# Filler products of a hybrid decoder kernel moved from the paired delta rule and its sample tile to the end of the chunked mixers

## The chip, the cores and the metric

The kernel runs on one core of one Trainium2 chip. The metric is the device time of one execution in microseconds (us); lower is better. All operands are float32.

## The reference, cut to what matters

One inference step of a trunk of two layers (DEPTH = 2) for 512 prompt tokens and 8 x 4 = 32 sample tokens, with width 1024. Each layer projects the tokens once and feeds four groups of heads, then mixes them, attends to a memory and applies an MLP:

```
z = x @ P['w_in']                               # 1024 -> N_IN, split among the groups
hm, C1, n1, m1 = _mlstm(...)                    # A: chunked matrix memory
ro, R1 = _retention(_rotary(rq), _rotary(rk), rv, R0)   # B: chunked retention
hg, h1, conv1 = _rglru(...)                     # C: gated linear recurrence
y_w, S1, shift1 = _rwkv7(...)                   # D: delta rule, per step
mix = concat([y_m, y_r, y_g, y_w]) @ P['w_out']
x = LN(ALPHA * x + mix); x = LN(ALPHA * x + cross_attn(x)); x = LN(ALPHA * x + mlp(x))
kp = mem_prompt @ xa_wk[l]; vp = mem_prompt @ xa_wv[l]   # memory keys and values
```

The delta rule D is, per head and time step, `S = S*w - (S kk) (kk*a)^T + v k^T; o = S r`. The kernel computes it in chunks of 64 tokens, with the inverse of a triangular matrix built by doubling.

## The kernel before, in words

**Tokens and tiles.** The 544 tokens are five tiles: T = 0 to 3 hold 128 prompt tokens each, T = 4 the 32 sample tokens. A projection column block f (128 output features) is kept as z(f), features on partitions, tokens along the row, and is made in two halves: 256 and 288 tokens.

**Two kinds of work on TensorE.** Every layer has a latency-bound stage, in which TensorE issues small matmuls for the groups D, A and B and waits between them for ScalarE, VectorE or GpSimd to turn their results into the next operands. To fill these waits the kernel holds back dense products that nothing near by needs and issues them in small portions: the fillers. They are needed work, listed in `SPARE` (line 708) in a fixed order: first 24 halves of z (slabs 4, 5 and 6 of `w_in`, column blocks 4 to 15), of 8 products each, then 16 halves of the memory keys and values (slabs 7 to 10, `xa_wk` and `xa_wv`), also of 8 products each. `spare_products` (line 723) issues the next ones at a named point of the program; its `units` count a z product (line 738, 128x256 or 128x288) as one and a key or value product (line 735, 128x512) as two. In the trace every product is two MATMUL records: one unit of z is two records of L738, two units of keys are two records of L735. The number of units at each point is written by hand:

- `FILL_OM` (3): ahead of the first level of an inverse (line 1076). `FILL_X` (5): at each level from m = 2 on (line 1090), between the product X and the products D and DT that need X back from ScalarE.
- lines 1055 and 1059 (3 and 5): while the scores of a tile of D are prepared, for each of the five tiles.
- line 1122 (3, and 1 for T = 4), line 1138 (1), `FILL_ST` (3, line 1146) and `FILL_SA` (2, line 1165): around the recurrence over the chunks.
- the sample tile of D, lines 1197 to 1247; then `FILL_D`, `FILL_BC`.
- `FILL_AB`: in the chunked mixers A and B, for each T, one portion between `front(T + 1)` and the scores of B (line 1421) and one after `outputs("A", T, 0)` (line 1424).
- `FILL_AB_S` (4): twice in each of the sample outputs of A and B (lines 1349 and 1353).

**Order of the work.** `delta_scores`, `delta_inverse`, `delta_states` run for the tile groups (0, 1), (2, 3) and (4,) (lines 1262 ff.). A paired group (g = 0, 1) inverts 8 heads x 2 chunks at once over the levels m = 1, 2, 4, 8, 16, 32; the sample tile (g = 2) has the levels 1 and 2. Level m begins with the product X (L1085), which needs a mask product of GpSimd (L2167) and the matrix Dm that VectorE writes (L1674 for m = 1, L1679 after it). ScalarE copies X back (L2022), TensorE makes D and DT (L1099, L1105), VectorE subtracts them (L1679, L1681). In the recurrence TensorE makes SA (L1155), VectorE turns it (L1699), TensorE uses it (L1173). For T = 4 VectorE also prepares the rotary embedding (L1609 to L1611) and spreads the values (L1724, L1726) that TensorE needs for the sample state (L1240).

In the mixers `outputs` for T = 4 multiplies the stored states with 4 tokens at a time: 32 records of 64x4 (L1345) for each half of the heads. A's needs the normalised output of the tile before (VectorE, L1803), whose PSUM bank it takes over.

**Banks and drains.** A filler half owns one PSUM bank from its first product until ScalarE has copied it out (L1922 for z, L1928 for keys and values). In the mixers all halves of keys and values use bank 3, so the first product of a half waits until the half before is copied. ScalarE looks for finished halves at fixed points (`spare_tiles`), in the order in which `HALF_DONE` says that they are finished.

**Loads.** SyncE issues the loads of the slabs into two ring slots, each when the slab two before it has been consumed (`slab_read`); these waits stand in SyncE's one queue, with the stores of states and the loads of the sample states between them.

Of the kernel before, what the change touches and what calls it, by code (L numbers as in the profile page):

```python
# [224 lines left out]
def build(nc, A, O, table, where):  # L225

    with ExitStack() as ctx:
# [130 lines left out]
        for l in range(DEPTH):  # L358
# [127 lines left out]
            UV = cols(tmp, dbase + 2048, H, HD)  # L486
# [224 lines left out]
            HALF_DONE = {}  # L711

            FILL_BONUS = 2 * KC
            FILL_OM, FILL_X, FILL_ST, FILL_SA = 3, 5, 3, 2
            FILL_4 = 4
            KV_BANKS = (0, 3)
            FILL_D = (4, 10)
            FILL_BC = 4
            FILL_AB = (6, ((6, 4), (10, 6), (10, 6), (10, 6)))
            FILL_AB_S = 4  # L720


            def spare_products(pe, point, units, banks, upto=None):

                at = HALF_DONE.get("at", 0)
                while at < len(SPARE) and (units > 0 if upto is None else at < upto):
                    n, f, half, k = SPARE[at]
                    key = ("kv", n - 7, half) if f is None else ("z", f, half)
                    if k == 0:
                        if half == 0 and (f is None or f == SLABS_IN[n][1]):  # L730
                            slab_pe(pe, n)
                        bk.begin(pe, key, banks[half] if f is not None or banks[0] == 3 else KV_BANKS[half])
                    bank = psum[:, bk.turn[key][0], :]
                    if f is None:
                        ins = pe.matmul(bank, memT[:, k, half * P:(half + 1) * P], wring[:, n % 2, k, :], start=(k == 0), stop=(k == KC - 1))  # L735
                    else:
                        c, i = HALVES[half][1], f - SLABS_IN[n][1]
                        ins = pe.matmul(bank[:, :c.stop - c.start], wring[:, n % 2, k, i * P:(i + 1) * P], xTv[:, k, c],  # L738
                                        start=(k == 0), stop=(k == KC - 1))
                    if k == KC - 1:  # L740
                        bk.filled(ins, key)
                    units -= 2 if f is None else 1
                    at += 1
                HALF_DONE["at"] = at
                HALF_DONE[point] = at // KC
# [214 lines left out]
            with nc.Block() as block:  # L960

                @block.tensor
                def _(pe):
# [40 lines left out]
                    for part, c in HALVES:  # L1004
                        w = c.stop - c.start
                        ps = bk.begin(pe, ("gates", "part", part), 4 + part)
                        for k in range(KC):
                            g = (k % 4) * NS
# [34 lines left out]
                    def delta_scores(T):  # L1043

                        t0, n = TILES[T]
                        dpad = dpads[T % 2]
                        own_chunks = CHUNKS if T < 4 else (slice(0, NS),)
                        pe.wait_ge(sig["dfeat"], sig.at("dfeat", 1))
                        for i, pair in enumerate(((X2, X4), (z(ZK_D, 2), z(ZV_D, 2)))):
                            ps = bk.begin(pe, ("dtok", T, i), (5, 7)[i]).rearrange("p (a c) -> p a c", a=4)  # L1050
                            for j in range(2):
                                for pr in range(2):
                                    ins = pe.transpose(ps[:n, 2 * j + pr, :], pair[j][:, pr, t0:t0 + n], ident)
                            bk.filled(ins, ("dtok", T, i))
                        spare_products(pe, ("dpad", T), 3, (0, 1))
                        pe.wait_ge(sig["dpad"], sig.at("dpad", 2 * (T + 1)))
                        for i, left in enumerate((X4, z(ZK_D, 2))):
                            if i:
                                spare_products(pe, ("dsc", T), 5, (0, 1))
                            ps = bk.begin(pe, ("dsc", T, i), (6, 4)[i]).rearrange("p (q a s t) -> p q a s t", q=2, a=2, s=2)  # L1060
                            for pr in range(2):
                                for c in own_chunks:
                                    tc = slice(t0 + c.start, t0 + c.stop)
                                    w = c.stop - c.start
                                    ins = pe.matmul(ps[c, pr, :, :, :w], left[:, pr, tc], dpad[:, pr, :, :, c], start=True, stop=True)
                            bk.filled(ins, ("dsc", T, i))


                    def delta_inverse(g):

                        tiles, levels = TILE_GROUPS[g], GROUP_LEVELS[g]
                        own_chunks = CHUNKS if g < 2 else (slice(0, NS),)
                        heads = range(H * len(tiles))
                        for li, m in enumerate(levels):
                            last = m == levels[-1]
                            spare_products(pe, ("om", g, m), FILL_OM if m == 1 or g == 2 else 0, (0, 1))
                            pe.wait_ge(sig["om"], sig.at("om", OM0[g] + li + 1))
                            ps = bk.begin(pe, ("X", g, m), 2).rearrange("p (h t) -> p h t", h=2 * H)
                            om = OmT[:, (OM0[g] + li) % 2]
                            if m > 1:  # L1080
                                bk.given(pe, ("X", g, 1) if m == 2 else ("D", g, m // 2))
                            for h in heads:
                                for c in own_chunks:
                                    w = c.stop - c.start
                                    ins = pe.matmul(ps[c, h, :w], om[c, h, :w], (const("ident64") if m == 1 else Dm[:, h, :])[c, :w],  # L1085
                                                    start=True, stop=True)
                            bk.filled(ins, ("X", g, m))
                            if m == 1:
                                continue
                            spare_products(pe, ("X", g, m), FILL_X, (0, 1))  # L1090
                            bk.given(pe, ("X", g, m))
                            if m > 2:
                                bk.given(pe, ("DT", g, m // 2))
                            if not last:
                                ps = bk.begin(pe, ("D", g, m), 3).rearrange("p (h t) -> p h t", h=2 * H)
                                for h in heads:
                                    for c in own_chunks:
                                        w = c.stop - c.start
                                        ins = pe.matmul(ps[c, h, :w], DmT[c, h, :w], Xm[c, h, :w], start=True, stop=True)  # L1099
                                bk.filled(ins, ("D", g, m))  # L1100
                            ps = bk.begin(pe, ("DT", g, m), 4).rearrange("p (h t) -> p h t", h=2 * H)
                            for h in heads:
                                for c in own_chunks:
                                    w = c.stop - c.start
                                    ins = pe.matmul(ps[c, h, :w], Xm[c, h, :w], DmT[c, h, :w], start=True, stop=True)  # L1105
                            bk.filled(ins, ("DT", g, m))


                    def delta_states(T):

                        t0, n = TILES[T]
                        dpad, Dtok, h0 = dpads[T % 2], Dtoks[T % 2], H * (T % 2)
# [6 lines left out]
                                ins = pe.matmul(ps[c, h, :], KM[c, h0 + h, 0, :c.stop - c.start],  # L1119
                                                Dtok[c, 3, h // 2, (h % 2) * HD:(h % 2) * HD + HD], start=True, stop=True)  # L1120
                        bk.filled(ins, ("CV", T))
                        spare_products(pe, ("inv", T), 3 if T < 4 else 1, (0, 1))
                        bk.given(pe, ("DT", T // 2, GROUP_LEVELS[T // 2][-1]))
                        if T < 4:
                            for cc, c in enumerate(CHUNKS):
# [9 lines left out]
                                for c in CHUNKS:  # L1135
                                    ins = pe.matmul(ps[c, 2 * (h % 2) + h // 2, :], DmT[c, h0 + h, :], CV[c, h, :], start=True, stop=True)
                            bk.filled(ins, ("UV", T))
                            spare_products(pe, ("UV", T), 1, (0, 1))
                            bk.given(pe, ("WK", T, 0))
                            bk.given(pe, ("WK", T, 1))  # L1140
                            bk.given(pe, ("UV", T))
# [186 lines left out]
                    def outputs(pre, T, bank):  # L1328
# [11 lines left out]
                        if T == 4:  # L1340
                            for pr in range(2):
# [6 lines left out]
                                if pr == 0:  # L1348
                                    spare_products(pe, ("ab", pre, 0), FILL_AB_S, (3, 3))
                            if pre == "A":  # L1350
# [65 lines left out]
                    key_scores("B", 0, 6)  # L1416
                    spare_products(pe, ("ab", 0, 0), FILL_AB[0], (3, 3))
                    for T in range(4):
                        outputs("B", T, 2)
                        front(T + 1)  # L1420
                        spare_products(pe, ("ab", T, 1), FILL_AB[1][T][0], (3, 3))
                        key_scores("B", T + 1, 6)
                        outputs("A", T, 0)
                        spare_products(pe, ("ab", T, 2), FILL_AB[1][T][1], (3, 3))
                    outputs("A", 4, 0)
# [907 lines left out]
            inv = cols(tmp, 10248, 4)  # L2333
# [894 lines left out]
```

## Time and profile before

| | |
|---|---|
| median of the runs | 2240.8 us (3 runs, 2239.32 to 2241.57) |
| profiled execution, its own time | 2243.67 us |
| span of the profiled execution | 2241.8 us |
| mean granted TensorE clock | 0.992 |
| TensorE busy with matmuls | 2188.2 us, 98% of the span |
| VectorE busy | 1167.9 us, 52% |
| ScalarE busy | 427.9 us, 19% |
| GpSimd busy | 113.0 us, 5% |
| DMA | 217.30 MB, mean 97 GB/s |

How to read it: times in a trace are us from the start of the span. PE is TensorE, DVE VectorE, ACT ScalarE, POOL GpSimd, SP SyncE. Matmuls are pipelined: a record's duration is longer than the distance to the next one, so neighbouring records overlap, and a busy PE is not a PE at its peak. What a group of records costs TensorE is the distance from its start to the start of the next group. "Granted clock" is the share of the full TensorE clock (2.4 GHz) that the chip granted; 0.50 is its lower level, 1.2 GHz. The latency-bound stage lies at 162 to 450 us in the first layer and at 1270 to 1556 us in the second.

### The profile page before, as it was taken

What the parts mean: (1) busy time and instruction counts of PE and PEld (TensorE: products, weight loads), DVE (VectorE), ACT (ScalarE), POOL (GpSimd) and SP (SyncE); (2) the same over time, 40 slices, a digit from 0 to 9 for tenths busy, and PEclk for the clock granted to TensorE, in tenths of its full rate; (3) what the DMA queues carried; (4) which work ended last, traced back from release to release, by engine and by line L of the source; (5) the groups of instructions that cost most, each with busy time, mean ns of one, the idle gap of its engine ahead of it and who ended that gap; (6) DMA issues with size and microseconds to landing.
All of it is one profiled execution on the core that took longest, in us unless ns stands there. A gap on an engine that the chain in (4) does not pass through costs nothing. (4 is left out here: it accounts for less than half of the span.)

```text
span 2241.8 us, 32592 instructions
## 1 busy us (share of the span) xinstructions
PE 2188.2 (98%) x13686; PEld 1638.0 (73%) x13686; DVE 1167.9 (52%) x1987; ACT 427.9 (19%) x899; POOL 113.0 (5%) x186
## 2 busy tenths in 40 slices
PE   7999999999999999999999999999999999999998
PEld 5877765547856888888988777655488478888888
DVE  5652236567466544675256422555765574448643
ACT  2332122021212221100023321221113022120000
POOL 0111101000000000000002111010001000000000
PEclk9999999899999999999999999998999999999999
DMA  7121124153542122222242111143335412223221
GB/s 275 64 76 40 32 66 124 55 176 131 189 169 94 48 103 76 75 76 75 76 134 76 38 41 59 43 124 111 115 150 208 158 67 76 76 76 106 82 75 41
DMA packets 136337, 217.30 MB, mean 97 GB/s; under 512 B 33672, under 2 KB 67776, under 8 KB 136064
## 3 DMA queue, kind: packets, MB, share of 16 engines
q1 hardware_dynamic: 133888, 211.02, 27.6%
q10 hardware_dynamic: 2304, 4.20, 0.5%
q8 instruction: 110, 1.80, 0.3%
q14 instruction: 35, 0.29, 0.0%
HBM read 198.39 MB, written 14.58 MB: 95 GB/s over the span
## 5 line engine op out<-in xcount | busy, mean ns | idle before, releaser
L738 PE MATMUL psum<-xT,ring 128*128 128x256 f32 (+1 forms) x768 | 203.5, 406 | 0.0
L2404 PE MATMUL psum<-tmp 128*128 128x272 f32 x768 | 181.2, 392 | 0.0
L2404 PEld LDWEIGHTS psum<-tmp 128*128 128x128 f32 x768 | 145.9, 190 | 30.1
L738 PEld LDWEIGHTS psum<-xT,ring 128*128 128x128 f32 x768 | 136.9, 189 | 34.4 <-issue 8.2
L735 PE MATMUL psum<-ring,ext 128*128 128x512 f32 x256 | 126.3, 629 | 1.6 <-ACT ext L1928 1.6
L688 PE MATMUL psum<-xT,ring 128*128 128x256 f32 (+1 forms) x512 | 120.4, 394 | 5.1 <-ACT big L1948 2.0
L2496 PE MATMUL psum<-big,ring 128*128 128x256 f32 (+2 forms) x768 | 119.9, 318 | 0.0
L2496 PEld LDWEIGHTS psum<-big,ring 128*128 128x128 f32 x768 | 112.4, 191 | 6.7
L688 PEld LDWEIGHTS psum<-xT,ring 128*128 128x128 f32 x512 | 96.3, 190 | 26.7 <-issue 5.0
L2404 PE MATMUL psum<-xT,ring 128*128 128x272 f32 x448 | 107.4, 393 | 0.0
L2404 PEld LDWEIGHTS psum<-xT,ring 128*128 128x128 f32 x448 | 85.0, 190 | 17.8 <-DMA ring<-in_w_up 0.3
L2448 PE MATMUL psum<-big,ring 128*128 128x272 f32 x384 | 91.6, 392 | 0.0
L844 PE MATMUL psum<-ring,big 128*128 128x512 f32 x192 | 85.5, 596 | 1.6 <-issue 1.6
L735 PEld LDWEIGHTS psum<-ring,ext 128*128 128x128 f32 x256 | 47.1, 197 | 51.0 <-issue 50.1
L2448 PEld LDWEIGHTS psum<-big,ring 128*128 128x128 f32 x384 | 72.6, 190 | 14.7
L338 DVE SCALAR_TENSOR_TENSOR xtok<-xtok,psum 128x256 f32<-128x256 f32 (+1 forms) x40 | 16.4, 410 | 104.6 <-PE psum L2394 102.6
L844 PEld LDWEIGHTS psum<-ring,big 128*128 128x128 f32 x192 | 35.8, 190 | 46.2 <-issue 45.6
L2448 PE MATMUL psum<-xT,tmp 128*128 128x272 f32 x288 | 68.6, 392 | 0.0
L2448 PE MATMUL psum<-tmp 128*128 128x272 f32 x288 | 68.0, 392 | 0.0
L1922 ACT ACTIVATE big<-psum 128x256 f32<-128x256 f32 (+1 forms) x80 | 31.7, 396 | 182.9 <-PE psum L688 100.0
L2404 PE MATMUL psum<-xT,tmp 128*128 128x272 f32 x256 | 64.0, 393 | 1.7 <-ACT xT L325 1.7
L2448 PEld LDWEIGHTS psum<-tmp 128*128 128x128 f32 x288 | 54.7, 190 | 11.3
(535 smaller groups left out, 3673.7 us busy)
## 6 DMA issues: line engine op xcount, KB each, us to landing
ring<-in_w_down SPq DMA_DIRECT2D x16, 2048.0 KB, 7.6
ring<-in_w_in SPq DMA_DIRECT2D x14, 2048.0 KB, 8.6
ring<-in_w_up SPq DMA_DIRECT2D x14, 2048.0 KB, 8.2
big<-in_cache_mem_k SPq DMA_DIRECT2D x16, 1024.0 KB, 7.7
ring<-in_xa_wk SPq DMA_DIRECT2D x4, 2048.0 KB, 9.0
ring<-in_xa_wv SPq DMA_DIRECT2D x4, 2048.0 KB, 11.7
ring<-in_w_out SPq DMA_DIRECT2D x4, 2048.0 KB, 8.7
ring<-in_xa_wq SPq DMA_DIRECT2D x4, 2048.0 KB, 10.5
```

The lines of the kernel that those rows point to most:

```text
L338: ins = v.scalar_tensor_tensor(x, x, ALPHA, ps[:n, at * W256:at * W256 + W256], ALU.mult, ALU.add)
L688: ins = pe.matmul(ps[:m, :w], lhsT_list[k], rhs(k)[:, c], start=(k == 0), stop=(k == n - 1))
L735: ins = pe.matmul(bank, memT[:, k, half * P:(half + 1) * P], wring[:, n % 2, k, :], start=(k == 0), stop=(k == KC - 1))
L738: ins = pe.matmul(bank[:, :c.stop - c.start], wring[:, n % 2, k, i * P:(i + 1) * P], xTv[:, k, c], start=(k == 0), stop=(k == KC - 1))
L844: ins = pe.matmul(ps, left(k), right[:, k, :], start=(k == 0 and i in (1, 2, 4, 5)), stop=(k == 3), skip_group_check=True)
L1922: bk.give(act(z(f)[:, c], ps[:, 0:c.stop - c.start], fn, scale=scale), ("z", f, half))
L2404: ins = pe.matmul(ps[:, :HT], left[:, k, :], right[:, k, :], start=(k == 0), stop=(k == KH - 1))
L2448: ins = pe.matmul(ps, left[:, k, :], right[:, k, :], start=(g == 0 and k == 0), stop=(g == 3 and k == KH - 1))
L2496: ins = pe.matmul(ps, w[r][:, k, i * P:(i + 1) * P], hT[:, 2 * KC * r + k, c], start=(r == first and k == 0), stop=(r != first and k == 2 ...
```

## The change

The numbers of units at the points change; nothing else does. The list of fillers, their order, their banks and their drains stay as they are, but each half is now begun and finished at other points.

```
-            FILL_OM, FILL_X, FILL_ST, FILL_SA = 3, 5, 3, 2
+            FILL_OM, FILL_X, FILL_ST, FILL_SA = 3, 4, 3, 1
...
-            FILL_AB = (6, ((6, 4), (10, 6), (10, 6), (10, 6)))
-            FILL_AB_S = 4
+            FILL_AB = (6, ((6, 4), (10, 6), (10, 6), (12, 12)))
+            FILL_AB_S = 6
...
-                        spare_products(pe, ("dpad", T), 3, (0, 1))
+                        spare_products(pe, ("dpad", T), 3 if T < 4 else 2, (0, 1))
...
-                                spare_products(pe, ("dsc", T), 5, (0, 1))
+                                spare_products(pe, ("dsc", T), 5 if T < 4 else 4, (0, 1))
...
-                            spare_products(pe, ("om", g, m), FILL_OM if m == 1 or g == 2 else 0, (0, 1))
+                            spare_products(pe, ("om", g, m), 2 if g == 2 or m == 2 else FILL_OM if m == 1 else 0, (0, 1))
...
-                            spare_products(pe, ("X", g, m), FILL_X, (0, 1))
+                            spare_products(pe, ("X", g, m), FILL_X if g < 2 else 2, (0, 1))
...
-                        spare_products(pe, ("inv", T), 3 if T < 4 else 1, (0, 1))
+                        spare_products(pe, ("inv", T), 2 if T < 4 else 1, (0, 1))
...
-                            spare_products(pe, ("UV", T), 1, (0, 1))
+                            spare_products(pe, ("UV", T), 2, (0, 1))
```

Counted along the list, per layer: 177 units of z products are issued before the sample tile's first state product in the old kernel and 156 in the new. From the portion ahead of the scores of B for T = 4 (line 1421, T = 3) to the end, 13 key and value products are issued in the old kernel and 24 in the new: 5, 3, 2, 2, 1, 0 at the six points become 6, 6, 3, 3, 3, 3.

## Rows read from the trace of the kernel before

**Rows 1.** The page: busy time of TensorE, and its granted clock in 40 slices.

```profile
PE 2188.2 (98%) x13686; PEld 1638.0 (73%) x13686; DVE 1167.9 (52%) x1987; ACT 427.9 (19%) x899; POOL 113.0 (5%) x186
PEclk9999999899999999999999999998999999999999
```

**Rows 2.** Waits of TensorE: who waited for whom, total us, times, longest.

```profile
PE psum L1345 <- DVE big L1803: 3.7, 2, 1.9
PE psum L1085 <- DVE tmp L1674: 3.5, 4, 0.9
...
PE psum L735 <- ACT ext L1928: 1.6, 2, 0.8
```

**Rows 3.** Windows, end of the stage in each layer; PEclk is the third number from the end.

```profile
426.00:460.00 34.00, 31.97 (x236) 18.17 (x232) 14.85 (x36) 3.20 (x6) 0.00 (x0) 0.75 0.30 97
1534.00:1566.00 32.00, 29.97 (x232) 17.18 (x228) 14.80 (x36) 2.88 (x5) 0.00 (x0) 0.79 0.31 104
...
433.00:442.00 9.00, 9.00 (x50) 4.93 (x49) 0.00 (x0) 0.00 (x0) 0.00 (x0) 0.50 0.01 2
...
447.00:452.00 5.00, 4.84 (x35) 3.95 (x34) 1.02 (x3) 0.71 (x2) 0.00 (x0) 0.50 0.92 311
```

**Rows 4.** Timeline of TensorE, first layer, end of the mixers: start, duration, what.

```profile
420.26 4.46 PE L735 MATMUL psum<-ring,ext 128*128 128x512 f32 x10
424.65 0.41 PE L1325 MATMUL psum<-big 128*32 128x64 f32 x4
...
427.27 2.84 PE L735 MATMUL psum<-ring,ext 128*128 128x512 f32 x6
431.98 1.49 PE L1345 MATMUL psum<-tmp 64*64 64x4 f32 x32 [1.87 <-DVE big L1803]
...
442.91 0.42 PE L1365 MATMUL psum<-xtok,tmp 32*64 32x32 f32 x8
...
444.03 1.10 PE L1345 MATMUL psum<-big 64*64 64x4 f32 x32
445.06 1.13 PE L735 MATMUL psum<-ring,ext 128*128 128x512 f32 x2
446.12 1.87 PE L1345 MATMUL psum<-big 64*64 64x4 f32 x32
...
448.71 3.99 PE L688 MATMUL psum<-big,con 128*128 128x256 f32 x8
```

**Rows 5.** Timeline, all engines, first layer: two levels of the paired inverse.

```profile
177.39 1.15 PE L1085 MATMUL psum<-con,xtok 64*64 64x64 f32 x32
...
179.42 1.15 PE L1085 MATMUL psum<-tmp,xtok 64*64 64x64 f32 x32 [0.88 <-DVE tmp L1674]
...
180.50 2.43 PE L738 MATMUL psum<-xT,ring 128*128 128x256 f32 x10
...
182.86 1.15 PE L1099 MATMUL psum<-tmp 64*64 64x64 f32 x32
...
186.04 2.69 PE L738 MATMUL psum<-xT,ring 128*128 128x288 f32 x10
186.14 0.60 ACT L2022 ACTIVATE tmp<-psum 128x512 f32<-128x512 f32 x1 [2.80 <-PE psum L1085]
...
188.66 1.15 PE L1099 MATMUL psum<-tmp 64*64 64x64 f32 x32
```

**Rows 6.** Timeline, all engines, first layer: the first chunk of the recurrence.

```profile
211.00 1.13 PE L738 MATMUL psum<-xT,ring 128*128 128x256 f32 x4
211.02 0.42 DVE L1699 SCALAR_TENSOR_TENSOR tmp<-psum,tmp 64x256 f32<-64x256 f32 x1 [2.96 <-PE psum L1155]
...
212.06 0.45 PE L1173 MATMUL psum<-tmp,xtok 64*64 64x64 f32 x8
```

**Rows 7.** Timeline, VectorE and TensorE, first layer: sample tile of D.

```profile
333.14 0.67 DVE L1726 TENSOR_TENSOR tmp<-xtok,con 32x512 f32<-32x512 f32 x1
333.87 1.07 PE L1240 MATMUL psum<-xtok 32*64 32x512 f32 x4 [0.79 <-DVE tmp L1726]
```

## The prediction

> **What bounds the kernel.** I read the page first. TensorE is busy for 98% of the span and everything else for half of it or less [rows 1], so only time in which TensorE stands still or runs slowly can be won. The slices show where it runs slowly: the clock has a 9 everywhere but for two slices with an 8, at about 400 and 1510 us, the end of the latency-bound stage in each layer [rows 1]. A 9 means 90% or more, so I asked for windows there. From 426 to 460 us the mean granted clock is 0.75, from 1534 to 1566 us it is 0.79; inside the first, two stretches stand at 0.50, the lower level of 1.2 GHz [rows 3]. The missing clock is 34 x 0.25 = 8.5 us and 32 x 0.21 = 6.7 us of TensorE time, 15.2 us in all.
>
> The list of waits gives the time in which it stands still. Those in the stage are few: 3.7 us in two waits for L1803, 3.5 us in four for L1674, 1.6 us in two for the drain of a half [rows 2]. The timeline puts them beside the clock: TensorE ends its six filler records at 430.1, stands for 1.87 us, issues the state products of 64x4, and runs at half clock from there. What takes 1.03 us at full clock (the 32 state products at 444.03) has a duration of 1.87 us instead of 1.10 at 446.12 [rows 4]. The clock is full again by 444, and falls a second time after 2.2 us of small products (442.9 to 445.06) with only two filler records behind them.
>
> **The change, part by part** (per layer; each edit acts in both).
>
> *The price of a unit.* Ten records of 256 take 2.36 us (180.50 to 182.86) and ten of 288 take 2.62 us (186.04 to 188.66) [rows 5]; four records of 256 take 1.06 us [rows 6]. So six records, three units, more cost 1.30 us: 0.43 us a unit at the margin, and 0.52 as the highest mean. I take 0.46, between the narrow and the wide halves. A key or value product at full clock: ten records take 4.39 us, two take 1.06 [rows 4], so 0.83 at the margin; 0.85 with the ends.
>
> *Units taken away ahead of the sample tile's state products.* One at each of ten X points, four at "inv", eight at SA and seven at T = 4: 29. Added: two at the second level of both paired inverses, one at each of four UV points: 8. Net 21 units, 9.7 us less (9.0 to 10.9). Is there cover?
> - X: the drain by ScalarE ends at 186.74, and TensorE goes on at 188.66 [rows 5]. The slack of 1.9 us bears one unit less; what is left is 1.4. Nothing is exposed.
> - SA: VectorE ends at 211.44 and TensorE goes on at 212.06 [rows 6]. Elsewhere TensorE starts 0.06 us after the end of the instruction it waited for (333.81 to 333.87 [rows 7]). With one unit less it would come at 211.60. Slack 0.1 us: exposed 0; 0.2 at each of eight chunks would be the upper end, 1.6 us. This is the thinnest cover in the change. What is late next if it fails is the state product, and behind it the whole recurrence.
> - inv, UV, T = 4: small steps on either side of a drain; I take 0, at most 1 us.
> - Second level: X(1) is issued in about 1.1 us of 2.03, then TensorE waits 0.88 us for L1674 [rows 5]. Two units fill this; they cost 0.92 and save 0.88. Twice a layer that is 1.8 us of idle time removed.
>
> So TensorE reaches the state products of the sample tile 9.7 + 1.8 = 11.5 us earlier.
>
> *Sample tile.* The units stay, but the list lags: they are z products until the point Sss, where before they were key products from SAs on. Per two units 0.92 stands against 0.85. Up to L1240 VectorE sets the time (it ends 333.81 [rows 7], TensorE waits 0.79), so this is absorbed; behind it ScalarE has the last z half, a table and two copies to do ahead of D's normalisation. I take +0.4 us, 0 to 1.5.
>
> *Drain waits.* In the old kernel one half ends in the middle of a portion of the mixers and its successor waits 0.8 us for bank 3 [rows 2]. By the list, the new portions cut at other products: that wait goes, and two others appear, in the twelve units after T = 3 and in A's second sample portion. Net +0.8.
>
> *Products added.* Eleven, from 13 to 24, at 0.85: +9.4 us. They are the same products that were taken away or passed over before, so no work is gained or lost.
>
> *The idle 1.87 us* [rows 4]. One product more ahead of B's scores delays VectorE's chain to L1803 by 0.85, and three more behind it delay TensorE by 2.5 us and 0.8 for the bank. 0.85 + 3.3 against 0.85 + 1.9: the wait is covered, 1.9 us saved.
>
> Without the clock a layer gives -11.5 + 0.4 + 0.8 + 9.4 - 1.9 = -2.8 us, two layers -5.6.
>
> *The clock.* It fell behind 1.9 us of idle and 0.5 us of state products. Now full products stand there, and 2.8 us of them on either side of each group of state products instead of 1.9, 1.9, 1.1 and none. If it never falls, 15.2 us come back; a few of the small products are not limited by the clock, so I take 14: -19.6 in all. But one stretch stays as it is: from A's last outputs to B's first states TensorE has 2.2 us of small products in a row, and behind that very stretch the clock fell in the old kernel [rows 3, 4]. There are now 2.8 us of full products behind it where there were 1.1. I expect it to fall in one layer of two; a fall like that from 446 to 453 costs 7 x 0.5, so 3.4 us: -16.2, say **-16 us**.
> *Loads.* SyncE asks for the slabs of keys, values and `w_out` later than before, against the products that use them, since each waits for a half of the slab two before. No wait of TensorE for such a load is among its waits in the stage, and SyncE's own queue has nothing between them that TensorE needs within a few us. I take 0, at most 2 us a layer.
>
> The Trainium skill, TensorE: Matmul & The Clock Gate, "Why this matters for your kernels", speaks against this part: it ties the loss of the full clock to long idle gaps between bursts, and the only gap here is shorter than those it warns of. By it the falls would have another cause, the filled gap would return only itself, and the time would be that of rival 1. The trace differs: the second fall has no idle gap ahead of it.
>
> The sum is made against the profiled execution, 2243.67 us (span 2241.8 and 1.9 around it): 2227.7. The median of the runs is 2.9 lower, 2240.8; so 2224.8.
>
> **The rivals.**
> 1. *The clock falls as before.* For it: the small stretch is unchanged, and nothing here shows what would hold the clock. Against it: 2.8 us groups of full products around state products of 1 us; the same mix in the sample tile of D runs at full clock in slices that show a 9 [rows 1]. Then only -5.6 is left: 2235.2.
> 2. *The fillers taken away turn into waits.* Place: SA in sixteen chunks and X at twenty levels. If all of those units came back as idle, 36 x 0.46 = 16.6 us are lost from 16: 2241. If only SA does, 7.4: 2232. For it: the slack of 0.1 at SA. Against it: 1.9 us at X.
> 3. *Slower: the clock falls in the delta rule.* Full products shrink there from 2.4 to 1.9 us between 3 us of 64x64 products, and at T = 4 from 20 to 13 units. Each fall costs 3.4 us, over 20 levels, 16 chunks and two sample tiles. It decides from five falls on (5 x 3.4 = 17 against 16); eight give 2252. Against it: at the second level there is 0.88 us of idle between two small groups and the clock stayed full [rows 5].
> 4. *No fall at all*, in both layers: 2221.2. It belongs to the forecast's own range, with two falls (2228) at its other end.
>
> **How the numbers follow.** Forecast, with no, one or two short falls: 0.64, 2220 to 2229. Rival 1: 0.14. Rival 2: 0.10, half of it at no change. Rival 3: 0.07. Something better than the sum, below 2219: 0.05. The range takes in the forecast, rival 1 and the cheap half of rival 2: 2219 to 2237. A measurement of this kernel can tell about 0.2% or 4.5 us from no change, so faster means below 2236.3: 0.64 + 0.05 + most of rival 1 (0.11) + half of rival 2 (0.05) = 0.85; within it 0.08; slower 0.07.
>
> **What would show it.** The list of waits has no L1345 <- L1803 and no L1085 <- L1674, L735 <- ACT doubles to four waits; L1155's neighbours show no wait for L1699. The window of 34 us ahead of the head means has a clock above 0.9 in at least one layer. L1240 of the first layer, which follows the sample tile's state products, starts at about 322.5 us instead of 333.87 [rows 7]. I am wrong if the clock there still has 0.75, if it falls between 160 and 330 us, or if waits for L1699 or L2022 stand in the list.

## The result, and the profile after

| | before | after |
|---|---|---|
| median of six runs each | 2241.2 us (2239.3 to 2250.2) | 2227.0 us (2224.8 to 2230.5) |
| ratio, with its 95% interval | | 0.9932 (0.9913 to 0.9951) |
| profiled execution, own time / span | 2243.67 / 2241.8 us | 2230.5 / 2228.7 us |
| mean granted clock of the profiled execution | 0.992 | 0.997 |

14 us less, where 16 were forecast. The whole interval of the ratio lies below 1, so the change is clear of the noise, though it is only 0.7%. The profiled execution is the slowest of its six, so its spans differ by 13.1 us only. The page of the changed kernel, against [rows 1]:

```profile
PE 2181.6 (98%) x13686; PEld 1636.7 (73%) x13686; DVE 1167.5 (52%) x1987; ACT 425.7 (19%) x897; POOL 113.0 (5%) x186
...
PEclk9999999999999999999999999999999999999999
```

The same 13686 records, and no slice with an 8. The waits of TensorE, against [rows 2]:

```profile
PE psum L735 <- ACT ext L1928: 2.9, 4, 0.8
PE psum L1119 <- ACT tmp L2040: 1.9, 4, 0.5
PE psum L1240 <- DVE tmp L1726: 1.8, 2, 0.9
PE psum L688 <- ACT tmp L2068: 1.0, 2, 0.5
```

The waits for L1803 (3.7 us) and L1674 (3.5 us) are gone; those for the drain L1928 went from two to four, +1.3 us; two short ones for L2068 behind the sample tile are new. The end of the mixers in the first layer, on TensorE, against [rows 4]:

```profile
409.87 5.32 PE L735 MATMUL psum<-ring,ext 128*128 128x512 f32 x12
...
420.49 3.67 PE L735 MATMUL psum<-ring,ext 128*128 128x512 f32 x8 [0.78 <-ACT ext L1928]
424.10 1.10 PE L1345 MATMUL psum<-tmp 64*64 64x4 f32 x32
425.12 2.84 PE L735 MATMUL psum<-ring,ext 128*128 128x512 f32 x6
427.90 1.10 PE L1345 MATMUL psum<-tmp 64*64 64x4 f32 x32
...
430.96 1.98 PE L735 MATMUL psum<-ring,ext 128*128 128x512 f32 x4 [0.69 <-ACT ext L1928]
432.88 0.42 PE L1365 MATMUL psum<-xtok,tmp 32*64 32x32 f32 x8
...
434.00 1.10 PE L1345 MATMUL psum<-big 64*64 64x4 f32 x32
435.02 2.84 PE L735 MATMUL psum<-ring,ext 128*128 128x512 f32 x6
437.80 1.10 PE L1345 MATMUL psum<-big 64*64 64x4 f32 x32
```

Where TensorE stood for 1.87 us, eight records run, and every group of 32 state products has its full-clock duration of 1.10 us. The windows over both ends, against [rows 3]:

```profile
420.00:454.00 34.00, 32.82 (x238) 17.71 (x239) 11.43 (x30) 6.51 (x12) 0.00 (x0) 1.00 0.53 175
1520.00:1552.00 32.00, 31.31 (x222) 15.46 (x220) 8.81 (x27) 2.87 (x5) 0.00 (x0) 0.89 0.45 153
```

The first layer has no fall at all, the second still has some. They show in the timeline as groups with too long a duration (second layer):

```profile
1421.26 1.07 PE L1240 MATMUL psum<-xtok 32*64 32x512 f32 x4 [0.92 <-DVE tmp L1726]
...
1423.12 5.73 PE L738 MATMUL psum<-xT,ring 128*128 128x256 f32 x16
```
```profile
1529.30 3.66 PE L735 MATMUL psum<-ring,ext 128*128 128x512 f32 x4 [0.69 <-ACT ext L1928]
...
1535.04 4.30 PE L735 MATMUL psum<-ring,ext 128*128 128x512 f32 x6
```

Sixteen records of 256 lasted 5.73 us, where ten take 2.36 at full clock [rows 5]; four records of 512 lasted 3.66 instead of 1.98 (at 430.96 above). What shows the low level in these two places is the full products behind the small ones, not the small ones ahead.

**Where the time came from.** I measure the stage from the first record of L1053 to the first of L844 (the output projection), and the time at half clock by adding up windows of 1 us. All rows of this table are sums of mine from timeline and windows.

| stage of | before | low clock in it | after | low clock in it |
|---|---|---|---|---|
| layer 1 | 162.12 to 463.00 = 300.9 us | 17.0 us | 163.83 to 454.20 = 290.4 us | 0 |
| layer 2 | 1269.96 to 1569.26 = 299.3 us | 13.6 us | 1261.26 to 1555.86 = 294.6 us | 10.2 us |

The stages give 10.5 + 4.7 = 15.2 us. Against it stands 1.7 us ahead of the first stage, where the change has no part (one group of L688 took longer in this execution), and 0.4 elsewhere: 13.1. The two stages of before differ by 1.6 us for 3.4 us of low clock: by my estimate one us at the low level costs 0.46. By that both have 293.0 us without any fall, and after has 290.4: 2.6 us a layer come from the edits themselves, 5.2 in all, and the other 10 from the clock. The 46 later runs of the kernel before give the price a second time: a line through their times and mean clocks has 0.43 us for each us at the low level, by which the edits have 6.2 us and the clock 9. So the split is an estimate, good to about a us. That the clock differs is not: none of these 46 runs has a mean clock above 0.994, and none of the twelve of the changed kernel (six here, six of its repeat) one below 0.997.

### The profile page after: what moved, and what is told of

The parts are those of the page before. It is cut to its first block and busy times, and to the rows that moved or that the text cites. A ratio compares the mean times of both kernels' runs of the same rounds, so it can differ in the third digit from the quotient of the medians.

```text
span 2228.7 us, 32592 instructions
## 1 busy us (share of the span) xinstructions
PE 2181.6 (98%) x13686; PEld 1636.7 (73%) x13686; DVE 1167.5 (52%) x1987; ACT 425.7 (19%) x897; POOL 113.0 (5%) x186
## 5 line engine op out<-in xcount | busy, mean ns | idle before, releaser
L738 PE MATMUL psum<-xT,ring 128*128 128x256 f32 (+1 forms) x768 | 207.3, 409 | 0.0
L688 PE MATMUL psum<-xT,ring 128*128 128x256 f32 (+1 forms) x512 | 122.8, 400 | 5.2 <-ACT big L1948 2.0
L688 PEld LDWEIGHTS psum<-xT,ring 128*128 128x128 f32 x512 | 98.3, 194 | 27.2 <-issue 5.0
L844 PE MATMUL psum<-ring,big 128*128 128x512 f32 x192 | 85.5, 597 | 1.6 <-issue 1.6
L844 PEld LDWEIGHTS psum<-ring,big 128*128 128x128 f32 x192 | 35.9, 190 | 46.1 <-issue 45.5
```

The source lines that it names most:

```text
L688: ins = pe.matmul(ps[:m, :w], lhsT_list[k], rhs(k)[:, c], start=(k == 0), stop=(k == n - 1))
L844: ins = pe.matmul(ps, left(k), right[:, k, :], start=(k == 0 and i in (1, 2, 4, 5)), stop=(k == 3), skip_group_check=True)
```

## The experiments

Two theories stood at first. **Small products:** the clock falls where TensorE issues small products with too few full ones between them, and comes back behind enough full ones. **Standing still:** it falls because of the idle 1.9 us, and filling that is what the change does. Ratios are to the kernel before, run on the same chip.

### The second level alone

```
-  spare_products(pe, ("om", g, m), FILL_OM if m == 1 or g == 2 else 0, (0, 1))
+  spare_products(pe, ("om", g, m), FILL_OM if m == 1 or g == 2 else 2 if m == 2 else 0, (0, 1))
-  spare_products(pe, ("X", g, m), FILL_X, (0, 1))
+  spare_products(pe, ("X", g, m), 3 if g < 2 and m == 2 else FILL_X, (0, 1))
```

> The kernel before with one part of the change alone: two units ahead of the second level of the two paired inverses, taken from the portion behind X of the same level (5 becomes 3), so that nothing else moves. My theory (the two units fill a wait that is there anyway): the four waits of L1085 for L1674, 3.5 us in all, are gone from the list, no new wait for ScalarE's copy L2022 appears, and each paired inverse is some 0.8 us shorter; 3 us less than before in all (2238), which is at the edge of what a measurement tells. Rival (the time comes back as the next wait, since the portion behind X was cover too): the waits for L1674 are gone, others of the same size stand behind X, and the inverse is as long as before.

2240.1 us (10 runs), ratio 0.9987 (0.9970 to 1.0004). The timeline shows the edit at work, against [rows 5]:

```profile
176.60 1.15 PE L1085 MATMUL psum<-con,xtok 64*64 64x64 f32 x32
177.68 1.13 PE L738 MATMUL psum<-xT,ring 128*128 128x256 f32 x4
178.74 1.15 PE L1085 MATMUL psum<-tmp,xtok 64*64 64x64 f32 x32
179.82 1.56 PE L738 MATMUL psum<-xT,ring 128*128 128x256 f32 x6
```

The wait of 0.88 us is gone and none took its place. No fall of the clock stands ahead of the sample tile in either kernel, so the gain can be read there directly: the first record of L1119 for T = 4 comes 149.5 us after the stage's start instead of 151.0, in both layers. That is 1.5 us a layer, a little less than the 1.8 of the two waits filled. The total can't show it: the ratio's interval takes in 1, since the clock's scatter is larger (here 13.6 and 10.2 us of low clock in stages of 297.5 and 295.3 us).

### The idle time covered, in the old kernel

```
-  FILL_AB = (6, ((6, 4), (10, 6), (10, 6), (10, 6)))
-  FILL_AB_S = 4
+  FILL_AB = (6, ((6, 4), (10, 6), (10, 6), (10, 10)))
+  FILL_AB_S = 2
```

> The kernel before, with the delta rule untouched: two products more in the portion ahead of the sample outputs of A, and one product instead of two in each of the portions between their state products, so that the standing time of 1.87 us ahead of L1345 is covered and the full products between the state products are fewer. My theory (the clock falls because TensorE does little in small products, not because it stands): the two waits for L1803 are gone, 3.7 us less; the clock still falls to its lower level at the end of the mixers in both layers, mean 0.85 or lower in the window that ends at the head means; 2236 to 2239 in all. Rival (it is the standing time that lets the clock fall): the clock stays full there in both layers, and with 3.7 and 14 us less the time is 2223 to 2226.

2239.0 us (10 runs, 2233.4 to 2253.3), ratio 0.9984 (0.9963 to 1.0005). TensorE's timeline and a window:

```profile
432.08 1.10 PE L1345 MATMUL psum<-tmp 64*64 64x4 f32 x32 [0.15 <-DVE big L1803]
433.11 1.13 PE L735 MATMUL psum<-ring,ext 128*128 128x512 f32 x2
434.16 1.26 PE L1345 MATMUL psum<-tmp 64*64 64x4 f32 x32
...
450.06 1.97 PE L1403 MATMUL psum<-big,tmp 32*64 32x512 f32 x4
451.96 2.18 PE L688 MATMUL psum<-big,con 128*128 128x256 f32 x4
```
```profile
435.00:468.00 33.00, 32.84 (x153) 18.00 (x152) 9.12 (x22) 5.36 (x9) 0.00 (x0) 0.50 0.40 113
```

The idle time is 0.15 us, TensorE is busy for 32.84 of 33 us, and the clock stands at half for 34 us. **A fall does not need TensorE to stand still.** The run does not say that idle time has no part: it also made the portions between the state products smaller. In this layer the clock stayed low all through the head means, although half of their time is full products (L688) and the other half small ones (L1403), and the stage took 307.8 us, 7 more than before. That is one execution and not a rule: in the same kernel's second layer, and in the kernel before, the clock was low at the start of the head means too and came back within them (at 1561 us here, at 453 us in the kernel before). The Trainium skill, TensorE: Matmul & The Clock Gate, "Why this matters for your kernels", puts such a loss down to long idle gaps between bursts of matmuls. The trace does not agree: this window has 0.16 us of idle time in all.

### Fillers taken from the mixers instead of the delta rule

```
-  FILL_BC = 4
-  FILL_AB = (6, ((6, 4), (10, 6), (10, 6), (10, 6)))
-  FILL_AB_S = 4
+  FILL_BC = 2
+  FILL_AB = (4, ((4, 2), (6, 6), (6, 6), (12, 12)))
+  FILL_AB_S = 6
```

> The delta rule and its sample tile as in the kernel before, the end of the mixers as in the changed kernel; the eleven products for the end are taken from the portions ahead of it (FILL_BC and the earlier FILL_AB). My theory (what counts is where the products go, not where they come from): the end of the mixers looks as in the changed kernel, clock 0.9 or more there; the four waits for L1674 stay, 3.5 us, and some new waits open where the portions shrank; 2229 to 2236. Rival (fewer fillers in the delta rule are what gains the time): within 3 us of the kernel before, 2238 to 2243.

2245.1 us (10 runs), ratio 1.0002 (0.9986 to 1.0017): my expectation fell. The wait for L1803 is gone as in the changed kernel and the end of the mixers has its fillers; the clock still falls there once in each layer (3.4 us each, at 439 and 1549 us), and for the larger part elsewhere: 10.2 us in the first layer and 20.5 in the second in all. Second layer, ahead of the chunk scores of the mixers:

```profile
1462.89 1.82 PE L735 MATMUL psum<-ring,ext 128*128 128x512 f32 x2
1464.64 2.18 PE L688 MATMUL psum<-big,con 4*128 4x256 f32 x4
1466.75 2.08 PE L735 MATMUL psum<-ring,ext 128*128 128x512 f32 x2
1468.76 2.18 PE L688 MATMUL psum<-big,con 4*128 4x256 f32 x4
```

Products from 4 partitions (L688) alternate with one full product each, and TensorE is at half clock for 17 us, busy all the time. So it matters where the fillers come from: taken from the mixers they open falls there. In the delta rule 4 records between two groups of 32 of 64x64 (at the second level, see above) keep the full clock, and none of the 13 traces of this study has a fall in a paired group.

### Two products in the small stretch

From A's last outputs to B's first states TensorE has 2.2 us of small products in a row; the prediction expected the remaining falls behind it. In the changed kernel two products were put inside, and taken from the two portions beside; the ScalarE look for the finished half moves with them.

```
+  spare_products(pe, ("ab", "M", 0), 4, (3, 3))       # between outputs of A and of B
-  spare_products(pe, ("ab", pre, 1), FILL_AB_S, (3, 3))
+  spare_products(pe, ("ab", pre, 1), 4, (3, 3))
-  spare_tiles(("ab", "A", 1))
+  spare_tiles(("ab", "M", 0))
```

> The changed kernel with one portion of two products moved into the 2.2 us of small products between the sample outputs of A and of B (A's and B's second portions give up one product each). My theory (that stretch is what still lets the clock fall): no window at the end of the mixers shows less than the full clock in either layer; the second layer's stage, 294.6 us in the profiled execution of the changed kernel, is 3 to 4 us shorter, the first's, 290.4 us, as long as it was; median 1 to 4 us below the changed kernel (2223 to 2226). Rival (the falls in the second layer come from elsewhere, the drain wait or the phase of the execution): the clock falls there as often as in the changed kernel, and the median is within 1 us of it.

2226.5 us (4 runs), ratio 0.9915 (0.9893 to 0.9937), the changed kernel's own time. One fall is left (first layer; the lines are one higher behind the insertion):

```profile
428.29 1.13 PE L735 MATMUL psum<-ring,ext 128*128 128x512 f32 x2 [0.69 <-ACT ext L1929]
...
430.46 3.50 PE L735 MATMUL psum<-ring,ext 128*128 128x512 f32 x4
```

Ahead of it stand the two groups of state products, a portion cut in two by the wait for its bank, and only then the stretch. My expectation fell and the rival's came: the stretch alone did not decide it.

### Portions cut where a half ends

The same, with the last portions ahead of the sample outputs 16 and 10 units instead of 12 and 12, A's first portion 6 units and B's first 4. So every half ends at the end of a portion, and its drain runs behind small products.

```
-  FILL_AB = (6, ((6, 4), (10, 6), (10, 6), (12, 12)))
+  FILL_AB = (6, ((6, 4), (10, 6), (10, 6), (16, 10)))
-  spare_products(pe, ("ab", pre, 0), FILL_AB_S, (3, 3))
+  spare_products(pe, ("ab", pre, 0), 6 if pre == "A" else 4, (3, 3))
```

> As x3_between, with the last portions of the mixers cut where a half ends (8, 5, 3, 2, 2, 2, 2 products), so that no half begins in the middle of a portion. My theory (the waits for bank 3 are paid in full, and with them gone and small products nowhere longer than 1.3 us in a row the clock stays up): the four waits of L735 for L1928, 2.9 us, are gone or below 0.5 us in all, no fall of the clock at the end of the mixers, each layer's stage 1.5 us shorter than the 290.4 us of the changed kernel without a fall; median 2222 to 2224. Rival (ScalarE's copy is late for another reason, or fewer products between the state products let the clock fall): the waits move to the start of the next portion, or a fall of 3.4 us and more shows in either layer, and the median stays at 2226 to 2228.

2222.2 us (6 runs, 2220.7 to 2223.7), ratio 0.9900 (0.9883 to 0.9917). The waits for L1928 are gone, no fall in either stage (288.8 and 288.7 us), and all six runs have a granted clock of 0.999. That leaves room for at most a short fall: the last 3 to 6 us of every profiled execution stand at the low level, outside the stages, and the repeat of the changed kernel has one fall of 3.4 us at a mean of 0.999. The group sizes are now 4 to 6 records between the state products, no more than in the changed kernel. Against the kernel of the section before (means of 0.997 to 0.999), what differs is that no wait cuts them; whether it is the cut or the 0.7 us of idle time in it that counts, no run separates.

### The cover at SA, and the idle time left open

Both start from the changed kernel: SA without any filler (its unit goes to the portion before), and a smaller portion ahead of B's scores so that part of the wait for L1803 returns.

```
-  FILL_OM, FILL_X, FILL_ST, FILL_SA = 3, 4, 3, 1
+  FILL_OM, FILL_X, FILL_ST, FILL_SA = 3, 4, 4, 0
```

> The changed kernel with the last unit behind SA taken away too (1 becomes 0) and put ahead of the next chunk (3 becomes 4). My theory (the change has used up the cover at SA to 0.1 us): sixteen waits of L1173 for L1699 of 0.4 to 0.5 us each appear, 6 to 8 us in all, and the time is 6 to 7 us above the changed kernel (2233). Rival (the cover at SA was still thick, or the unit ahead of the chunk makes good for it): waits below 0.1 us each and the time of the changed kernel, 2227.

```
-  FILL_AB = (6, ((6, 4), (10, 6), (10, 6), (12, 12)))
+  FILL_AB = (6, ((6, 4), (10, 6), (10, 12), (12, 6)))
```

> The changed kernel with the portion ahead of the sample outputs of A back at three products (the three others go one tile earlier), so that the standing time ahead of L1345 is open again while the portions between the state products stay at three. It is the counterpart of x2_idle_covered. My theory (the full products between the state products hold the clock, the standing time only costs itself): two waits for L1803 of 1 to 2 us each are back, one or two more drain waits, the clock at the end of the mixers falls no more than in the changed kernel; 2 to 6 us above it (2229 to 2233). Rival (the standing time lets the clock fall): falls right behind L1345's wait in both layers, and 10 us above it or more.

SA bare: 2230.4 us (4 runs), ratio 0.9934 (0.9908 to 0.9961). Its waits:

```profile
PE psum L1173 <- DVE tmp L1699: 7.0, 16, 0.8
```

0.44 us at each of sixteen chunks. The stages grew by 2.5 and 2.1 us over a clean one of the changed kernel (290.4), less than the 3.5 us of waits in each, since eight portions fewer have to be started: 0.13 to 0.17 us for each start by this difference, 0.2 by that at the sample tile, which comes 2.0 and 1.8 us later. The kernel is 4.6 us slower by its stages, not the 6 to 7 expected. In the first two chunks L1173 starts 0.82 and 0.79 us after the last group of L1162 where it waits for VectorE, and 1.01 and 0.95 us after it in the changed kernel: the one unit that the change leaves at SA covers VectorE with 0.16 to 0.19 us to spare. No fall came of the waits.

Idle time open: 2231.0 us (5 runs), ratio 0.9940 (0.9920 to 0.9960). In the first layer TensorE stands still and keeps the full clock:

```profile
426.58 1.10 PE L1345 MATMUL psum<-tmp 64*64 64x4 f32 x32 [1.05 <-DVE big L1803]
427.61 2.84 PE L735 MATMUL psum<-ring,ext 128*128 128x512 f32 x6
```

Its stage of 292.5 us without a fall is 2.1 above the changed kernel's: the 1.05 us of idle time and 0.7 us more of drain waits. An idle us costs a us here, not a fall. The second layer, with the same wait of 1.05 us, fell twice (3.4 us each), but later: the first of the two began 7 us behind that wait and 0.2 us behind a wait of 0.69 us for L1928.

### The changed kernel again, and its end undone

> The changed kernel once more, for a second profile and more times on this chip. My theory (the falls that are left depend on where the small products happen to stand, so they differ from one execution to the next): another number or place of falls than in the first profile (none in layer one, two of 3.4 us at the end of layer two, one of 3.4 us in its sample tile); each layer's stage is 290.4 us plus about half of the time at the lower level; median 2225 to 2229. Rival (they are fixed by the program): the same three falls at the same instructions.

2225.8 us (6 runs, 2224.8 to 2231.0), ratio 0.9919 (0.9901 to 0.9937). In this execution layer 1 has no fall (290.4 us) and layer 2 one, at 1422 us in the sample tile (291.3 us): 3.4 us at the low level that cost 0.9 us, less than the 1.6 that 0.46 would give. The two falls at 1529 and 1536 of the first profile are not there. So where small products leave the clock on the edge, one execution falls and the next does not, and one trace is a sample.

The second kernel keeps the delta rule's edits and restores the old end:

```
-  FILL_AB = (6, ((6, 4), (10, 6), (10, 6), (12, 12)))
-  FILL_AB_S = 6
+  FILL_AB = (6, ((6, 4), (10, 6), (10, 6), (10, 6)))
+  FILL_AB_S = 4
```

> The delta rule and its sample tile as in the changed kernel, the end of the mixers as in the kernel before; what is left over of the fillers (eight products) is issued in one go behind B's sample outputs. My theory (taking the fillers out of the delta rule gains nothing by itself but frees them for the end): the waits for L1674 stay gone, the waits for L1803 are back with 3.7 us, and the clock falls at the end of the mixers in both layers; 2233 to 2239. Rival (the end of the mixers needs only some full products behind it, wherever they stand): the two waits are back, the clock stays up, 2228 to 2231.

2230.6 us (4 runs), ratio 0.9937 (0.9915 to 0.9960). I expected more, the waits for L1803 are 2.1 us in all and not 3.7, and the clock fell at the end of one layer, not of both. The four runs with their mean clocks: 2225.7 (0.999), 2228.3 (0.997), 2232.8 and 2233.3 (0.995). The one at 0.999 costs what the changed kernel does. In the profiled one, first layer:

```profile
420.12 1.10 PE L1345 MATMUL psum<-tmp 64*64 64x4 f32 x32 [1.05 <-DVE big L1803]
421.15 2.85 PE L735 MATMUL psum<-ring,ext 128*128 128x512 f32 x4
423.93 1.88 PE L1345 MATMUL psum<-tmp 64*64 64x4 f32 x32
...
440.91 7.13 PE L735 MATMUL psum<-ring,ext 128*128 128x512 f32 x16 [0.81 <-ACT ext L1928]
```

The second layer has the same products in the same order behind the same wait, and the full clock throughout:

```profile
1524.94 1.10 PE L1345 MATMUL psum<-tmp 64*64 64x4 f32 x32 [1.05 <-DVE big L1803]
1525.97 1.98 PE L735 MATMUL psum<-ring,ext 128*128 128x512 f32 x4
1527.88 1.10 PE L1345 MATMUL psum<-tmp 64*64 64x4 f32 x32
```

So groups of four records between the state products do not decide by themselves whether the clock falls. What decided between the two layers is not shown.

The products taken out of the delta rule arrive at the end in any case: with fewer consumed before, the old numbers leave every point in the outputs its two products, where [rows 4] show one at 445.06, and the rest is issued behind B (the sixteen records at 440.91). Its stages, 296.9 and 291.3 us with 13.6 and 3.4 us of low clock, would be near 290 without it, as the changed kernel's. By the medians the new end is worth 4 to 5 us (2230.6 against the changed kernel's 2227.0 and 2225.8), but with four runs the intervals of the ratios overlap, so this is not clear of the noise.

### Two steps further

On top of the portions cut at halves: more units ahead of L1240 where TensorE waited 0.92 us for VectorE, fewer behind it.

```
-  spare_products(pe, ("SX", pr), 2 * FILL_4, (0, 1))
+  spare_products(pe, ("SX", pr), 10 - 2 * pr, (0, 1))
-  spare_products(pe, ("bc", q, pr), FILL_BC, (0, 1))
+  spare_products(pe, ("bc", q, pr), FILL_BC if q * pr == 0 else 2, (0, 1))
```

> x5_cut_at_halves with one product of the fillers more in the sample tile: ten units instead of eight ahead of the first state product of D's sample tile, where TensorE waits 0.9 us for VectorE (L1726), and one key product less behind the last of the four broadcasts. My theory (that wait is VectorE's time and can hold two units; the half of z that ends there also no longer stands ahead of ScalarE's work for D's norm): the two waits for L1726 and the two for L2068 are gone, 2.8 us; each stage 1.2 to 1.5 us shorter than the 288.8 us of x5_cut_at_halves; 2219 to 2220.5. Rival (the chain is VectorE's all through, so the time comes back at the next wait for it, L1734): the waits for L1734 grow by as much, 2222.

2221.6 us (5 runs), ratio 0.9901 (0.9882 to 0.9919), no less than the 0.9900 of the portions cut at halves, so a gain shows in the stages alone. Both waits it aimed at are gone, and another is there:

```profile
PE psum L1325 <- DVE xtok L1780: 1.1, 2, 0.5
```

The stages are 0.7 us shorter, not 1.4: behind the sample tile VectorE's chain is late next.

```
+  spare_products(pe, ("cv", T), T % 2, (0, 1))        # ahead of CV
-  spare_products(pe, ("inv", T), 2 if T < 4 else 1, (0, 1))
+  spare_products(pe, ("inv", T), 2 - T % 2 if T < 4 else 1, (0, 1))
```

> x10_sample_tile with one of the two units behind CV put ahead of it for T = 1 and 3, where TensorE waits 0.5 us for the drain of the output before it (L1119 for L2040, four times, 1.9 us). My theory: the unit fills the wait, what remains behind CV is still enough for VectorE's copy; 1.5 to 1.9 us below x10_sample_tile. Rival (the unit was cover behind CV): waits of L1130 or L1136 of the same size appear, no gain.

**2218.6 us** (5 runs, 2217.8 to 2220.8), ratio 0.9889 (0.9872 to 0.9906). The 1.9 us of waits of L1119 for ScalarE (L2040) are gone, and no wait of L1130 or L1136 took their place; the stages are 287.5 and 287.3 us, 0.7 us shorter each. The medians differ by 3.1 us, more than the 1.4 of the stages and the 1.5 to 1.9 expected; the rest is not explained. This is the fastest kernel of the study, some 8 us below the changed one, and by the ratio 25 below the one before.

## Why the prediction was right

Forecast 2224.8 us, measured 2227.0 and, in the repeat, 2225.8. By its steps:

- **Units ahead of the sample tile, -9.7, and second level, -1.8: 11.5 us earlier.** The first record of L1119 for T = 4 came 139.4 us after the stage's start instead of 151.0, and L1240 160.1 instead of 171.8: 11.6 each. The second level by itself gave 1.5 us of its 1.8. The time named for L1240, 322.5, came as 323.97, 1.5 later; the stage itself began 1.7 later in this execution.
- **SA, exposed 0, slack 0.1.** No wait for L1699. Without the last unit 0.44 us a chunk are exposed; the thinnest cover of the change held, with 0.16 to 0.19 us in it instead of 0.1.
- **Sample tile, +0.4.** A new wait of 0.5 us for L2068 in each layer stands behind it, as the step said (ScalarE has the z half to drain first). The rest of it can't be separated.
- **Drain waits, net +0.8.** Two became four, 1.6 became 2.9 us: +0.65 a layer. What I did not see is that they also cut the groups of full products, and that the clock stayed up once they were gone.
- **The idle 1.87 us, -1.9.** Gone. With the other terms -2.8 us a layer was forecast; -2.6 came by the price of 0.46, -3.1 by 0.43.
- **The clock.** Its price was right: 14 us were taken, (17.0 + 13.6) x 0.46 = 14.1 by the two stages. What is left was taken as one fall of 7 us that costs 3.4; the profiled execution lost 4.2 us (294.6 against 290.4) to three falls of 3.4 us, the repeat 0.9 to one. So the amount is near, but it is made up of shorter and cheaper falls. The place was only half right. One of the three came behind the small stretch that I named, one behind the drain wait ahead of it, one in the sample tile behind L1240.
- **The reason given for it was half right.** I began with "it fell behind 1.9 us of idle and 0.5 us of state products". The covered idle time with 34 us of low clock, and the open idle time with none in one layer, show that idle time is neither needed for a fall nor enough for one; whether it adds to one is open, and the waits that cut the portions point that way. That larger groups of full products hold the clock fits all runs but is not shown by itself: with the old end restored, the same groups fell in one layer and not in the other.

**The rivals.** *Clock as before* (2235.2) fell: the windows show 1.00 and 0.89 instead of 0.75 and 0.79. *Waits at SA or X* fell; there are none. *Falls in the delta rule* from five on: one, in the sample tile of one layer, and the kernels that left the old sample tile alone show such a fall too (at 340, 336 and 337 us in three of them). Its price was too high as well: 3.4 us a fall, where the one in the sample tile of the repeat cost 0.9. The prediction took the sample tile for safe because its slice of the page shows a 9; a slice is 56 us long, and a fall of 3.4 us takes only 3% of its clock, so a 9 can't exclude one. *No fall at all* (2221.2) was some 3 us too low: runs of the changed kernel with a mean clock of 0.999 gave 2224.8 to 2227.5, and the profiled one of 2224.9 had one fall of 0.9 us.

**The step that was furthest off** is the last of the sum, the 2.9 us from the profiled execution down to the median. The 46 later runs show that the old kernel's times follow the clock (2239 to 2242 us at 0.994, 2242 to 2245 at 0.992), and the profiled execution was one with 0.992. The 14 us of clock came from that execution, so most of the 2.9 was in them already and was taken off twice. Without it the sum stands at 2227.7 and the case without a fall at 2224.1, where the measurements are. With it the forecast of 2224.8 is 1 to 2 us too low. That these 2.9 us are clock is worked out from the scatter, not seen in a trace.

By four runs with the old end restored, the new distribution at the end is worth some 4 us by itself, and the larger part of the 10 us from the clock comes with the products merely reaching the end of the stage; the overlap of the intervals leaves that split open.

## What to carry to other kernels

Look for a low granted clock in the windows even where the engine is busy all the time. What follows is what worked in this kernel, tried at the places named above and nowhere else: put filler products first between groups of small ones that use a corner of the array (64x4, 4 partitions, 32 wide), take them from where the small products are 64x64 and come 32 at a time, and cut the portions where a buffer is handed over, so that no wait splits them. Judge such a change by several executions and their clocks: the trace of one shows whether it can fall, not how often.

## What the runs showed that I had not expected

- **Falls come in one size.** In the stages every one lasted 3.4 us, or two, three, five or ten times that. What a us of it costs depends on the place: 0.46 us by the two stages of the kernel before and 0.43 by its 46 runs, but 0.26 in the sample tile of the repeat.
- **The scatter is the clock.** Beside the steps named above, the kernel before took 2247 to 2248 us at a mean clock of 0.991, 2249 to 2250 at 0.989 and 2253.5 at 0.987. The last two versions hold 0.999 in all ten runs, within 1.4 and 3 us. An edit that holds the clock takes away the scatter as well as time.
- **Low clock can last.** 34 us in one layer, through all the head means; in the same kernel's other layer the clock was low where the head means begin as well, but the fall was over after 6.8 us, and the stage was 13.5 us shorter. What made the difference is open.
- **A portion has a price of its own**, 0.13 to 0.2 us for its start. Eight portions of one unit cost over 1 us a layer before they cover anything.
